# One program of slots for the opening and the index scores, and cached keys that load inside the projection

## The reference, cut to what matters

```python
h = rms_norm(x, norm_g) * (1 + scale(c)) + shift(c)
iq, ik, iw, fa = columns of h @ ab_w_in       # 8 heads x 64, 64, 8, 8
iq, ik = apply_rope(iq), apply_rope(ik)
rel   = relu(einsum('bqhd,bkd->bqhk', iq, ik))
score = einsum('bqh,bqhk->bqk', iw * SCALE, rel)   # over the 8 heads
logf  = log_sigmoid(fa + f_bias); cum_f = cumsum(logf)
sel   = top_k(score, n_sel)
```

## Time and profile before

| | |
|---|---|
| median of 3 runs | 1878.53 us (1875.09 to 1881.5) |
| profiled execution: its own time | 1881.4 us |
| span in the profile | 1879.6 us |
| PE busy | 1685.7 us (90% of the span), granted clock 0.949 |
| DVE busy | 1276.7 us (68%) |
| ACT busy | 806.8 us (43%) |
| POOL busy | 226.5 us (12%) |

### The profile page before, as it was taken

How to read it: one execution, slowest core, us unless ns; L and a number is a source line. 1 busy time by engine, 2 the same in 40 slices (tenths; PEclk the granted TensorE clock), 3 DMA queues, 4 the chain that set the end, 5 groups by cost and what they waited for, 6 DMA issues and landing times. The chain is left out here.

```text
span 1879.6 us, 34318 instructions
## 1 busy us (share of the span) xinstructions
PE 1685.7 (90%) x12878; PEld 1314.9 (70%) x12878; DVE 1276.7 (68%) x2807; ACT 806.8 (43%) x1750; POOL 226.5 (12%) x310
## 2 busy tenths in 40 slices
PE   4984899999999967889998998998987999999798
PEld 1762567777888855667776787787875776777687
DVE  2653766887988946678888655636546777777764
ACT  3514632221112115668886325512216677777421
POOL 2221000000000104010000000010005222220000
PEclk6986989999999988899998998999998999999899
DMA  9226235654234129967764643423334111111432
GB/s 328 69 59 127 72 118 135 196 180 156 81 113 129 50 67 247 233 202 201 213 197 135 232 168 124 118 86 109 91 75 91 35 39 28 29 37 44 160 132 101
DMA packets 222421, 235.17 MB, mean 125 GB/s; under 512 B 122714, under 2 KB 156354, under 8 KB 221235
## 3 DMA queue, kind: packets, MB, share of 16 engines
q1 hardware_dynamic: 215378, 213.07, 39.7%
q0 software_dynamic: 6880, 19.92, 2.8%
HBM read 173.98 MB, written 58.95 MB: 124 GB/s over the span
## 5 line engine op out<-in xcount | busy, mean ns | idle before, releaser
L579 PE MATMUL PS<-ab_wh,hT 128*128 128x512 f32 x576 | 231.9, 403 | 3.8 <-DVE ab_wl L930 3.8
L580 PE MATMUL PS<-ab_wl,hT 128*128 128x512 f32 x576 | 226.4, 393 | 0.0
L581 PE MATMUL PS<-ab_wh,hT 128*128 128x512 f32 x576 | 225.8, 392 | 0.0
L1377 DVE TENSOR_SCALAR_CACHE_REDUCE topk_junk<-scores,topk_small 128x528 bf16<-128x528 f32 (+6 forms) x224 | 194.6, 915 | 1.3
L2588 DVE CUSTOM_DVE_ANT_0 la_S<-PS,la_mask 128x128 f32<-128x128 f32 (+3 forms) x144 | 107.5, 747 | 41.5 <-PE PS L581 28.5
L579 PEld LDWEIGHTS PS<-ab_wh,hT 128*128 128x128 f32 x576 | 108.8, 189 | 31.5 <-issue 5.8
L888 ACT ACTIVATE ab_nat<-PS 128x512 f32<-128x512 f32 x54 | 32.2, 596 | 229.7 <-PE PS L581 229.7
L581 PEld LDWEIGHTS PS<-ab_wh,hT 128*128 128x128 f32 x576 | 108.7, 189 | 24.9
L580 PEld LDWEIGHTS PS<-ab_wl,hT 128*128 128x128 f32 x576 | 108.8, 189 | 21.6
L579 PE MATMUL PS<-out_wh,out_mT 128*128 128x512 f32 x288 | 116.4, 404 | 4.7 <-DVE out_mT L2038 4.7
L1735 ACT ACTIVATE at_P<-at_S,at_nm 128x128 f32<-128x128 f32 (+2 forms) x144 | 110.5, 767 | 17.3 <-DVE at_nm L1780 17.2
(11 more groups left out here) (424 smaller groups left out, 4285.5 us busy)
## 6 DMA issues: line engine op xcount, KB each, us to landing
ab_wl_raw<-in_ab_w_in SPq DMA_DIRECT2D x64, 256.0 KB, 5.2
mod_w<-in_ada_w SPq DMA_DIRECT2D x32, 512.0 KB, 4.0
out_g<-scratch_gates_nat SPq DMA_DIRECT2D x18, 512.0 KB, 5.6
mod_ada_w<-in_ada_w SPq DMA_DIRECT2D x8, 1024.0 KB, 10.2
at_kc<-in_cache_a_k SPq DMA_DIRECT2D x8, 1024.0 KB, 8.6
at_vc<-in_cache_a_v SPq DMA_DIRECT2D x8, 1024.0 KB, 9.4
at_kc<-in_cache_b_k SPq DMA_DIRECT2D x8, 1024.0 KB, 5.4
at_vc<-in_cache_b_v SPq DMA_DIRECT2D x8, 1024.0 KB, 5.4
```

Of the source, the lines that this page charges most:

```text
L579: nc.tensor.matmul(out, x[0], w[0], start=start, stop=False)
L580: nc.tensor.matmul(out, x[0], w[1], start=False, stop=False)
L581: return nc.tensor.matmul(out, x[1], w[0], start=False, stop=stop)
L1377: go(V.tensor_scalar(mark, x, limit, 0.0, op, ALU.add, accum_out=cnt[:, m:m + 1]), 0 if m == M - 1 else 1)
```

## The change

`opening` and `index_scores` become one block. The order is nine slots. In slot p PE turns the rows at place p+3, multiplies tile `Q_TILES[p]` (slots 0 to 6) and makes the scores of tile `Q_TILES[p-2]` (slots 2 and 4 to 8), in the order of `CHUNKS`. Cut to its core (`PS[:, 0, :]` is one PSUM bank):

```diff
-IX_ORDER = [("q", 0), ("q", 1), ("s", 0), ("q", 2), ("s", 1), ("q", 3), ("s", 2), ("s", 3), ("q", 4), ...
-X_RING = 6
+ROWS = [2, 0, 1, 8, 3, 4, 5, 6, 7]
+X_RING = 4
+AHEAD = 3
+Q_TILES = [2, 8, 3, 4, 5, 6, 7]
+Q_LAG = 2
+SPAN_AT = {0: 0, 3: 1, 5: 2}
+CHUNKS = ("c0", "c1", "keys", "query", "c2", "c3", "s0", "c4", "s1", "c5", "s2", "c6", "s3", "c7", "span", "s4", "s5", "narrow", "s6", "s7")
...
+    first = at(chosen[-2], 4)
+    turn_at = {first + 3 * (b // 2) + b % 2: b for b in range(NB)}
+    score_at, sum_at = {s + 3: b for s, b in turn_at.items()}, {s + 5: b for s, b in turn_at.items()}
+    CACHE_ROW, SUMS_ROW, NEW_ROW, SCAN = first - 4, first - 2, N - 4, N - 1
...
@@ tensor
-            turn_rows(1)
-            for kind, i in IX_ORDER:
+            turn_rows(1)
+            turn_rows(2)
+            for p in range(SLOTS):
+                if p + AHEAD < NT:
+                    turn_rows(p + AHEAD)
...
+            def multiply(p, n):
+                    if p:
+                        pe.wait_ge(q_nat, p)
+                last = product(nc, PS[:, 0, :], ...)
+            def score(s):
+                for u, (a, w) in enumerate(pieces(i), units[s]):
+                    if u >= 3:
+                        pe.wait_ge(relu_done, u - 2)
+                    for d in range(2):
+                        last = nc.tensor.matmul(PS[:, bank(u), 0:w], q[...], k[:, d, a:a + w], ...)
@@ scalar, one relu for each piece of up to 512 columns, two buffers
+                if s >= 2:
+                    act.wait_ge(acc_done, s - 1)
+                for u, (a, w) in enumerate(pieces(i), units[s]):
+                    nc.scalar.activation(rel[:, s % 2, a:a + w], PS[:, bank(u), 0:w], ACT.Relu)
@@ vector, three tiles at once
+            def narrow_keys(n):
+                tiles = slice(3 * n, 3 * n + 3)
@@ sync
-                sp.dma_start(c.s["iqT"]..., T...)            # every tile to DRAM
+                        sp.dma_start(q[...], T[...])         # prompt tiles from SBUF to SBUF, four DMAs
@@ class Modulation
-        self.w = stack.enter_context(nc.sbuf_tensor("mod2_w", [P, 2, D], F32))
+        self.w = c.spare[:].rearrange("p (a b) d -> p a (b d)", a=2)
     def finish(self, sp):
         sp.wait_ge(self.gate_out, 128)
+        sp.wait_ge(self.mod_T, 1)
+        sp.dma_start(self.c.spare[:], self.c.i["cache_a_k"][0, 0]...).then_inc(store_semaphore("first_keys"), 16)
@@ projection, sync
+                    if s == side.PLACE_AT + 2:
+                        side.finish(sp)
...
-            if side:
-                side.finish(sp)
@@ branches_ab, sync
-                sp.dma_start(kc[:, g % 2], ...).then_inc(kc_in[g % 2], 16)
+                if g:
+                    sp.dma_start(kc[g % 2][:], ...).then_inc(kc_in[g % 2], 16)
```

More of the change, by code:

```diff
@@ new lines, in opening @@
+    steps = [(i, h) for i in chosen for h in range(H)]
+    N = len(steps)
+    pieces = lambda i: [(a, min(512, (i + 1) * P - a)) for a in range(0, (i + 1) * P, 512)]
+    units = [0]
+    for i, h in steps:
+        units.append(units[-1] + len(pieces(i)))
+    bank = lambda u: 5 + u % 3
+    slot_tile = lambda p: Q_TILES[p - Q_LAG] if 0 <= p - Q_LAG and Q_TILES[p - Q_LAG] < QT else None
+    n_span = lambda p: sum(1 for q in SPAN_AT if q <= p)
+    nk, BH = PAST // P, NB * H
+    at = lambda i, h: chosen.index(i) * H + h
@@ L114, in opening @@
[L114 to L118, removed]
@@ L160, in _ @@
[L160 to L172, removed]
@@ L223, in squares @@
                 act.wait_ge(x_in[n], 16 * len(tiles))
[L224 to L227, removed]
+                for p in tiles:
+                    if p:
+                        act.wait_ge(sq, p)
+                    nc.scalar.activation(junk[:], x[:, p % X_RING, :], ACT.Square, accum_out=rstd[:, ROWS[p]:ROWS[p] + 1]).then_inc(sq, 1)
@@ L294, in _ @@
+            for s in range(N, END):
+                sample_step(s)
+            act.wait_ge(new_done, 1)
+            nc.scalar.activation(rs_new[:].rearrange("p b t -> p (b t)"), PS[:, 0, 0:P], ACT.Relu).then_inc(new_read, 1)
         @block.vector
@@ new lines, in multiply_span @@
+            def multiply_span(n):
+                ready = max(place[i] for i in range(3 * n, 3 * n + 3)) + 1
+                if n == 0:
+                    pe.wait_ge(small_lo, 1)
+                else:
+                    pe.wait_ge(k_lo, n)
+                pe.wait_ge(hi_done, ready)
+                pe.wait_ge(lo_done, ready)
+                for b in range(KT):
+                    last = product(nc, PS[0:SMALL, 4, 0:SPAN], [sh[:, b, :], sl[:, b, :]],
+                                   [h[:, b, n * SPAN:(n + 1) * SPAN] for h in hT], b == 0, b == KT - 1)
+                last.then_inc(across_done, 1)
@@ L488, in _ @@
-            turn_s(NT - 1)
-            turn_q(NT - 1)
+            turn_rows(2)
+            for p in range(SLOTS):
+                if p + AHEAD < NT:
+                    turn_rows(p + AHEAD)
+                i = slot_tile(p)
+                for chunk in CHUNKS:
+                    if chunk[0] == "c" and p < len(Q_TILES):
+                        multiply(p, int(chunk[1]))
+                    if chunk == "keys" and p - 1 in SPAN_AT:
+                        turn_keys(SPAN_AT[p - 1])
+                    if chunk == "query" and 0 <= p - 1 < len(Q_TILES):
+                        turn_query(p - 1)
+                    if chunk == "span" and p in SPAN_AT:
+                        multiply_span(SPAN_AT[p])
+                    if chunk == "narrow" and p in SPAN_AT:
+                        turn_narrow(SPAN_AT[p])
+                    if chunk[0] == "s" and chunk != "span" and i is not None:
+                        s = at(i, int(chunk[1]))
+                        score(s)
+                        sample(s)
@@ new lines, in _ @@
+            for s in range(N, END):
+                sample(s)
+            pe.wait_ge(rel_read, NB)
+            for b in range(NB):
+                qb = [qs[:, d, b].rearrange("d h t -> d (h t)") for d in range(2)]
+                last = product(nc, PS[:, 0, b * TS:(b + 1) * TS], qb, [kn[:, d, b * TS:(b + 1) * TS] for d in range(2)], True, True)
+            last.then_inc(new_done, 1)
+            pe.wait_ge(new_read, 1)
+            for b in range(NB):
+                last = weighted(b, 4, TS, rs_new[:, b, :])
```

968 lines of the change are left out of this document (489 added, 479 removed).

## The result

| | before | after |
|---|---|---|
| median | 1880.01 us (1875.09 to 1881.7, 4 runs) | 1821.44 us (1819.91 to 1824.61, 4 runs) |
| ratio | | 0.969, 95% interval 0.9671 to 0.9709 |
| profiled execution | 1881.4 us, span 1879.6 | 1824.61 us, span 1822.8 |
| PE busy, granted clock | 1685.7 us, 0.949 | 1658.0 us, 0.958 |
| DVE busy | 1276.7 us | 1263.3 us |

A forecast was written before the change was run, and what follows sets the result against it. Opening bound by PE's columns, index scores by the PE, ACT, DVE round trip, seam by transfers. 1881.4 - 40.0 (projection's start) - 2.5 (attention's first keys) = 1838.9, less 2.9 for the median: 1836.0 us; range 1804 to 1862.

The forecast's parts named there:

- case A: Whole kernel: the forecast itself, 1836 us, own range 1824 to 1848, chance 0.50.
- step 6: Attention's start: early load of the first keys saves 2.5 us, taken between 0 and 3.7.
- Step 1: Opening: first index product starts at 61.2 us, 13.0 us later, after the row at place 3 is turned.
- Step 2: Slots 0 to 6 of the merged block: end at 152.9 us, slots 2 to 6 lasting 68.9 us.
- Step 3: Slots 7 and 8: seam 6.7 us without a step, then 16 steps of tiles 6 and 7 in 35.5, to 195.1.
- the signs: Marks to confirm the forecast, among them some 6 us with neither product nor step near 153 us.
- Step 4: Tail before the projection: four half-empty steps 3.7 us, new keys to first split 7.4 us, to 206.2.
- Step 5: PE's clock before the projection: one fall counted, costing 2.9 us, so the projection starts at 209.1.
- B: Opening and index scores: PE bound throughout as waits melt together, start 183.6, time 1810.5 us; chance 0.20.
- Rival C: Opening and scores: DVE in strict order is the bound, slots 2 to 6 take 87.8 us, time 1855; chance 0.21.
- D: Opening and scores: PE's clock stays down; with half the work at half clock, 1892.5 us; chance 0.05.
- E: Whole kernel: no net change, the merged block's gain lost in another stage or no overlap, 1878.5 us; chance 0.04.

The follow-up runs named there:

- run 9: Changed kernel with the fourth tile's transposes moved behind slot 0's product chunks in PE's order: 1814.57 us, ratio to before 0.9646.
- run 2: Kernel before with only the spare buffer and head 0's cached keys loaded early, in the projection: 1873.13 us, ratio 0.9944.
- run 1: Changed kernel with the load of head 0's cached keys put back in the attention: 1823.2 us, ratio to before 0.9691.
- run 8: Kernel before with 35 small products on PE: 1869.92 us; counterpart, changed kernel with the keys' load back in the attention and 29: 1833.59 us against 1823.2.
- Run 4: Kernel before without seven eighths of the index products of tiles 0 and 1: 1868.21 us, projection starting at 244.41 us.

## Why the prediction was right and where it was wrong

The sign and the stated range were right, and the opening went as case A has it. The time was 14.6 us too high by the medians and lies 2.6 us below A's own range of 1824 to 1848. By the profiles the gain is 14.3 us over the forecast: 13.1 in the attention (step 6) and 2.5 at the start of the projection, less the 1.4 us (rounded) that the rest gave back. Point by point:

- **Step 1**, right. Forecast 61.2, measured 61.15, by the chain that I had followed. That PE could have been working meanwhile I did not ask; run 9 shows 6.9 us there.
- **Step 2**, right. The second slot ends at 82.82 (forecast 84.0), slots 2 to 6 end near 153.2 (152.9). The narrow product's wait was 2.39 us (3.3).
- **Step 3**, right in sum. The three waits of the seam are 6.6 us (6.7). The steps with batches end some 2 us later than the 195.1 forecast: the last sums of batches start at 197.39, the new keys at 199.23, where steps 3 and 4 gave 198.8. (28.7 us at 80% are 35.9, not the 35.5 of the step; this is small beside the 2 us.) The seam isn't one stretch of 6 us, as the signs had it, but three waits with steps between them.
- **Step 4**, right: 7.3 us from the new keys to the projection's first product (7.4).
- **Step 5** can't be told apart. The start of 209.1 held 2.9 us for one fall of the clock; measured 206.54, and the steps without it give 206.2. The clock did fall behind the wait of 2.39 us, to 0.83 over 100 to 110 us. A mean of 0.95 over 61 to 153 us means some 9 us at half clock, which is 4 to 5 us of PE work (my estimate), and step 2 held 1.8 of them. So the clock cost something, and other terms were as much too high; that the start came out within 2.6 us is in part luck.
- **Step 6** failed: 2.5 us forecast, 15.6 measured. It had taken the attention's gain to be the wait for the keys, bounded by what is late next. Two things were missing. The keys can be worth more than their wait: in the kernel before, their early load brought about 8 us by the medians (run 2), in the changed one 1.8, inside the spread (run 1). And the larger part is no property of the load: PE runs 56 products less ahead of the attention (12,878 against 12,822), and this alone moves where its code is cut into pieces. Its price was measured from both sides: 8.8 us gained in run 8 and 10.4 lost in its counterpart by the medians, 8.3 and 8.0 in the stage, of the 15.6. The bounds of the step, 0 and 3.7, thus left out the case that came. Nothing in it was unreadable: the four issue waits 21 us apart stood in the timeline of before.
- **Rivals** of the prediction. B needed a PE without waits, and had the start at 183.6. From 170 to 200 us PE was 98% busy, but the seam and slot 0 weren't. Rival C (not the theory C of the experiments) had slots 2 to 6 at 87.8 us and steps of over 2.7 us in the last two tiles. The slots took 70.4. The steps took 2.2 us on average, from DVE's first sum at 161.59 to its last at 194.92, though the last eight stand 2.7 apart, at the edge of that sign. D: the clock was 0.95 over slots 0 to 6 and 1.00 from 170 to 200 us. The Trainium skill's rule on micro-idles between bank-cycled groups ("TensorE: Matmul & The Clock Gate", "A second HAM failure mode: psum-queue depth-cycling") doesn't describe this stage, whose steps cycle three banks at full clock. E fell with all of it.

What stays open: how much of the opening's 42.5 us is dropped work and how much overlap. Run 4 gave 4.65 us for 8.9 us of PE work that was dropped alone, without the two tiles' work on DVE. It is open also why run 2 falls in two groups of times, and why a late piece of code costs PE 4 us at one instruction and nothing at another.

## What to carry to other kernels

Where the DMA engines are full and one engine runs several hundred instructions in 20 us, look for its waits of kind "issue" at even distances: there its code may come late, and an edit anywhere ahead can move the time by 0.5% with no change in work. So judge an edit stage by stage, with the marks of a timeline, before its gain is put down to what it was meant to do; and test a suspected shift with padding in idle time, counted on the page rather than in the source. At the head of an in-order queue ask what behind it could already run: one moved line gave 6.9 us here by the medians, 5.6 of it by the start of the projection.

## What the hardware showed that I had not expected

- A piece of PE's code (16.3 KB) that arrives while the DMA engines are full (share 0.86 to 1.09 in and just before the waits of the kernel before) can stop PE for 2.0 to 6.1 us (the last in the kernel before with 70 small products), and PE's clock is then below full in the stretch: 0.93 over 120 us, against 1.00 where the pieces fall better.
- 35 additional small products at the kernel's start made it 8.8 us faster by the medians, 10.5 by the ratio.
- A 128x32 f32 product of the identity counts twice on PE's page (70 gave 140, 128 gave 256, 35 gave 70).
- One and the same load moved out of the attention was worth 8 us by the medians in one kernel and 1.8 us in the other; four runs with a spread of 8 us don't show that the two differ.
